# Merged cache runs, stacked new values and a finer last output in a hybrid attention decoder step

## The chip, the cores and the metric

The kernel runs on one core of a Trainium2 chip. The metric is the device time of one execution in microseconds, the median of several runs. TensorE (PE in the rows) multiplies matrices, ScalarE (ACT), VectorE (DVE) and GpSimd (POOL) work element by element, and SyncE (SP) issues nearly all transfers. The engines run side by side and wait for one another through semaphores.

## The reference

Two layers are applied to 320 tokens of width 1024: one prompt of 256, and eight samples of 8 tokens, each with a cache of 2048 earlier positions. Each layer does

```python
x = x + 0.5 * swiglu_1(rms(x))
z = rms(x) @ w_in                 # q, k, v of 3 dilated groups, of the sink attention, and 2 gates
A = dilated window attention      # (window, dilation) = (128,1), (512,4), (2048,16); 4 heads each,
                                  # the groups' heads weighted by their softmax denominators
B = window attention of 128       # 8 query heads on 2 key heads, with a learned sink per head
x = x + (sigmoid(gA) * (A @ w_branch_a) + sigmoid(gB) * (B @ w_branch_b)) @ w_out
x = x + 0.5 * swiglu_2(rms(x))
```

and after both a final norm follows. The attention of a sample goes over rows of its caches and over its 8 new keys and values. The outputs are y and all window caches, shifted by the new rows. All is in fp32.

## The kernel before, in words

Activations lie transposed, features on the partitions and 320 tokens along the free axis. A weight matrix is split into a rounded part and a rest (whi, wlo), as is the activation, and three matmuls of 320 columns make one product (L632 to L635). Weights come in units of eight 128x128 tiles: SP loads `raw` (L490), ACT rounds it (L1022), DVE takes the rest (L1244), and PE uses the unit. DVE's rest of unit n + 4 is made in step n, and SP loads the raw tile of unit v when the rest of unit v - 4 is done.

The mixer of a layer is written out by hand. `mixer_steps` (L118) makes one list of steps, and every engine walks it in order and does its share of each step. Step ("U", u) is unit u of w_in, 24 products on PE. `BEATS` (L111) says which pieces of attention follow unit u: S scores, T transposed probabilities, O values; the number is the item (0 to 3 prompt items of the dilated groups, 4 and 5 the sample items SA of these groups by half of the samples, 6 to 9 prompt items of the sink attention, 10 its sample item). S1a and S1b are two parts of a score. `TILES` (L114) says how many cache tiles follow unit u. There are 52 in a layer: 26 of keys (step K, `cached_keys`, 8 matmuls each) and 26 of values (step V, `cached_values`, 4 matmuls each), 13 for each half of the samples. They are small matmuls whose results have 32 rows, four of which lie side by side on the array.

The order in a step matters below. PE does unit u, then the beats, then the tiles. ACT empties the unit (`zs`, L1110), rounds a weight unit, copies transposed probabilities (L1179), and does the exponentials of a score (L1144) when DVE has found the maxima. POOL scales `zs` into `t1` (L1577). For a query or key unit DVE shuffles, multiplies and adds (L1334, L1338, L1341; the last signals `rope_done`). DVE also makes the maxima (L1410), the rest of a weight unit (step w) and the scaling of the exponentials (step N, L1442). Token rows of unit u - 3 (step R) are transposed in the middle of unit u, and ACT copies them out (L1122 to L1129).

Four waits of PE are named below. In the last key tile of the first half (tile 12, counted from 0) PE also multiplies the queries with the new keys, and for that it waits for the rotated keys of unit 14:

```python
if i == CT - 1 and half == 0:
    pe.wait_ge(rope_done, L * 17 + 12)       # L865
```

The first value tile of the second half (tile 39) waits until ACT has copied the sums of the first half out of PSUM, which is step Y, placed in the list behind tile 38:

```python
if half == 1 and i == 0:
    pe.wait_ge(osb_done, L * 2 + 1)          # L893
```

The values of an item of the dilated groups wait for the token rows of its value units (L811). And each tile waits for its load (`kvc_wait`). Loads go to a ring of `KV_RING` places; `cache_load_places` (L172) puts the load of tile n in SP's order seven units behind the step that uses tile n - KV_RING, and there SP waits until that tile is used.

The new values of the samples are summed in `values`: for an SA item 3 groups by 4 samples, 12 matmuls with 32 rows of `vnew` (L845). At the end DVE makes y in four parts of two of the eight feature chunks (L1513), and SP stores each (L620).

Of the kernel before, what the change touches and what calls it, by code (L numbers as in the profile page):

```python
# [7 lines left out]
F32 = mybir.dt.float32  # L8
# [5 lines left out]
P = 128  # L14
# [31 lines left out]

LOADS = (("x", 0), ("a", 0), ("x", 1), ("a", 1), ("x", 2), ("b", 0), ("x", 3), ("b", 1), ("w", 2), ("w", 3))
XPARTS = 4
HALF_UNIT = UT // 2 * P

START_RUNS = ((0, (0, 1)), (0, (2, 3)), (1, (0, 1, 2, 3)), (0, (4, 5)), (1, (4, 5)), (0, (6, 7)), (1, (6, 7)))
# [39 lines left out]
SA0 = ITEMS.index(("SA", 0, 0))  # L91
TWO_PARTS = [i for i, _i in enumerate(ITEMS) if _i[0] == "A" and _i[2] == 1]
SINKED = [i for i, _i in enumerate(ITEMS) if _i[0] in ("B", "SB")]
KV_RING = 5
KST = 3
T1 = 3
QK_GATES, QK_GATE0 = 12, 5
# [8 lines left out]
def parts(i):  # L106
# [1 line left out]

BEATS = {10: "S0", 12: "T0 S1a", 13: "S1b", 14: "O0", 15: "T1a", 16: "T1b S2", 18: "T2 O1 S3a", 19: "S3b", 20: "O2",  # L111
         21: "T3a", 22: "T3b S4", 23: "O3", 24: "T4 S5", 26: "T5 O4 S6", 27: "O5", 28: "T6 S7", 30: "T7 O6 S8",
         32: "T8 O7 S9", 34: "T9 O8 S10", 36: "T10 O9", 38: "O10"}
TILES = {10: 4, 12: 4, 14: 3, 16: 2, 18: 4, 20: 4, 22: 3, 23: 2, 26: 4, 28: 4, 30: 5, 32: 4, 34: 4, 36: 5}  # L114
FILL_Q = 6


# [122 lines left out]
def build(nc, a):  # L240
    ctx = ExitStack()
    with ctx:
# [37 lines left out]
        with ExitStack() as att:  # L280
            kvc = sb("kvc", [P, KV_RING, NB * P], F32, att)
            vb = sb("vb", [P, NB, P], F32, att)
            kb = sb("kb", [P, NB * P], F32, att)
            qm_mem = sb("qm_mem", [P, 2 * 4 * CT * HALF], F32, att)
            qk = sb("qk", [P, 17, TOK], F32, att)
            vtok = sb("vtok", [P, 2, 7 * P], F32, att)
            vnew = sb("vnew", [HALF, 2, 7 * P], F32, att)
            kst = sb("kst", [P, KST, 3 * P], F32, att)

            e = sb("e", [P, 2 * NG * SEQ], F32, att)
            pts = sb("pts", [P, 2 * NG * SEQ], F32, att)
            ptn = sb("ptn", [HALF, 4 * P], F32, att)

            sts = sb("sts", [P, N_SA], F32, att)
            osb = sb("osb", [P, 2 * P], F32, att)
            t1 = sb("t1", [P, T1, TOK], F32, att)
            cosr = sb("cosr", [P, TOK], F32, att)  # L300
            sinr = sb("sinr", [P, TOK], F32, att)
            mx = sb("mx", [P, 4], F32, att)
            nmx = sb("nmx", [P, 4], F32, att)
            den = sb("den", [P, 4], F32, att)
            esk = sb("esk", [P, 4], F32, att)
            nsk = sb("nsk", [P, 4], F32, att)
            rden = sb("rden", [P, 4], F32, att)
# [131 lines left out]
        def skips_first_rows(u):  # L439

            kind, g, _ = COLS[u]
            return kind == "k" and g in (0, 3)

        def new_place(first, count):

            return BK_T + 1, slice(first * P, (first + count) * P)
# [29 lines left out]
        def _(sp):  # L476
# [53 lines left out]
            def store_kv(L, n):  # L530

                kind, g, c = COLS[KV_UNITS[n]]
                name = ("a1", "a2", "a3", "b")[g]
                kv = 0 if kind == "k" else 1
                heads = P * c
                sp.wait_ge(kvtok_done, L * 14 + n + 1)
                if kind == "k":
                    nk = K_UNITS.index(KV_UNITS[n])
                    src, done = kst[:, nk % KST, 0:2 * P].rearrange("p (t f) -> p t f", t=2), kst_out[nk % KST]
                    parts = [(slice(0, NB), kst[0:NB * NT, nk % KST, 2 * P:3 * P])]  # L540
                else:
                    cols = slice(v_slot(g, c) * P, (v_slot(g, c) + 1) * P)
                    src, done = vtok[:, :, cols], v_out
                    parts = [(slice(4 * half, 4 * half + 4), vnew[:, half, cols]) for half in range(2)]
                t0 = 0 if g in (1, 2) else 1
                dst = a[f"new_{name}_prompt"].rearrange("l n (t p) v h d -> l p (n t) v (h d)", p=P)
                dst = dst[at(L), :, :, kv, heads:heads + P].rearrange("l p t f -> (l p) t f")
                sp.dma_start(dst, src[:, t0:2, :]).then_inc(done, 16)
                dst = a[f"new_{name}_sample"]
                w = dst.shape[2]  # L550
                dst = dst[:, :, w - NT:w, :, :, :].rearrange("l b t v h d -> l b t v (h d)")
                for batches, new in parts:
                    to = dst[at(L), batches, :, kv, heads:heads + P].rearrange("l b t f -> (l b) t f")
                    sp.dma_start(to, new).then_inc(done, 16)
# [55 lines left out]
            for L in range(DEPTH):  # L610
# [3 lines left out]
                    sp.dma_start(sinks[:, :, :], a["sinks"]).then_inc(const_in, 16)  # L614
                mixer_loads(L)
                ffn_loads(L, 1)
            for n in range(XPARTS):
                m = slice(n * KD // XPARTS, (n + 1) * KD // XPARTS)
                sp.wait_ge(y_done, m.stop)
                sp.dma_start(a["y"][:, m, :], x[:, m, :]).then_inc(y_out, 16)  # L620
            sp.wait_ge(y_out, 16 * XPARTS)
            sp.wait_ge(copy_out, 16 * DEPTH * (4 * 2 * NB + 2 * KD + 4 * 2))
            sp.wait_ge(v_out, DEPTH * 7 * 48)
            for n in range(KST):
# [4 lines left out]
        def _(pe):  # L629
# [89 lines left out]
            def mixer_products(L):  # L719
# [48 lines left out]
                def transposes(i, part):  # L768
# [13 lines left out]
                    elif kind == "B":  # L782
                        for n in range(4 * (t + 1)):
                            j, kt, cc = n // (2 * (t + 1)), n // 2 % (t + 1), n % 2
                            o = (2 * j + cc) * (t + 1) * P + kt * P
                            mm = pe.transpose(ps[:, BK_T + n // 4, n % 4 * P:(n % 4 + 1) * P], e[:, o:o + P], ident)
                    else:
                        for n in range(4 if kind == "SB" else NG):
                            o = n * N_SB if kind == "SB" else n * P
                            on = n * N_SB + P if kind == "SB" else NG * P + n * HALF  # L790
                            pe.transpose(ps[:, BK_T, n * P:(n + 1) * P], e[:, o:o + P], ident)
                            mm = pe.transpose(ps[0:HALF, *new_place(n, 1)], e[:, on:on + HALF], ident)
                    mm.then_inc(s_pt, 1)

                def values(i):
# [25 lines left out]
                    elif kind == "SB":  # L821
                        pe.wait_ge(vb_in, L * 16 + 16)
                        pe.wait_ge(kvtok_done, L * 14 + 14)
                        for h in range(2):
                            for j in range(2):
                                r, n = slice(HD * j, HD * (j + 1)), 2 * j + h
                                pe.matmul(ps[r, BK_O, h * P:(h + 1) * P],
                                          vnew[:, h, 6 * P + HD * j:6 * P + HD * (j + 1)],
                                          ptn[:, n * P:(n + 1) * P], start=True, stop=False)
                            for b in range(4):  # L830
                                for j in range(2):
                                    r, n = slice(HD * j, HD * (j + 1)), 2 * j + h
# [5 lines left out]
                    else:  # L838
# [1 line left out]
                        pe.wait_ge(s_masked, L * NI + SA0 + 2)  # L840
                        pe.wait_ge(kvtok_done, L * 14 + 12)
                        plain(pe)
                        for g in range(NG):
                            for b in range(4):
                                mm = pe.matmul(ps[HALF * b:HALF * (b + 1), BK_KV, 2 * P * c:2 * P * (c + 1)],  # L845
                                               ptn[:, g * P + HALF * b:g * P + HALF * (b + 1)],
                                               vnew[:, c, v_slot(g, 0) * P:(v_slot(g, 0) + 2) * P],
                                               start=g == 0 and c == 0, stop=False, skip_group_check=True)
                        mm.then_inc(s_new, 1)

                def cached_keys(n):
# [165 lines left out]
        def _(act):  # L1017
# [80 lines left out]
            def mixer_act(L):  # L1098
                act.wait_ge(const_in, 32)
                for kind, n in STEPS:  # L1100
# [11 lines left out]
                    elif kind == "R":  # L1112
# [12 lines left out]
                        else:  # L1125
                            v0 = v_slot(g, c) * P
                            nc.scalar.activation(vtok[:, :, v0:v0 + P],
                                                 ps[:, BK_ROWS, 0:2 * P].rearrange("p (t f) -> p t f", t=2), ACT.Copy)
                            nc.scalar.activation(vnew[:, :, v0:v0 + P],  # L1129
                                                 ps[0:HALF, BK_ROWS, 2 * P:4 * P].rearrange("p (t f) -> p t f", t=2),  # L1130
                                                 ACT.Copy).then_inc(kvtok_done, 1)
                    elif kind == "G":
                        k = G_UNITS.index(n)
                        act.wait_ge(t1_done, L * N_IN + n + 1)
# [14 lines left out]
                    elif kind == "T":  # L1149
# [5 lines left out]
                        if what == "SA":  # L1155
                            if h == 0:
                                act.wait_ge(pm_zero, L + 1)
                            else:
                                act.wait_ge(s_new, L * 2 + 1)
                            nc.scalar.activation(ptn[:, 0:NG * P], ps[0:HALF, *new_place(0, NG)], ACT.Copy)  # L1160
                            src = ps[:, BK_T, :]
                            by_tile = ((0, ((CT * HALF, 4), (1, HALF))),
                                       (HALF, ((CT * HALF, 4), (4, 2 * 4), (HALF + 1, 4))),
# [8 lines left out]
                        else:  # L1172
                            if part == 0 and users:
                                wait_item_out(act, L, users[-1])
                            if what == "SB":
                                act.wait_ge(s_new, L * 2 + 2)
                                nc.scalar.activation(ptn[:, :], ps[0:HALF, *new_place(0, 4)], ACT.Copy)
                            w = {"A": 2 * NG * P, "B": 4 * (t + 1) * P, "SB": 4 * P}[what]
                            nc.scalar.activation(pts[:, part * w:(part + 1) * w], flat[:, 0:w], ACT.Copy)\  # L1179
                                .then_inc(s_pts, 1)  # L1180
# [59 lines left out]
        def _(dve):  # L1240
# [267 lines left out]
                .then_inc(diag_done, 1)  # L1508
            dve.wait_ge(spread, 1)
            dve.wait_ge(xhi_done, (3 * DEPTH + 1) * KD)  # L1510
            for n in range(XPARTS):
                m = slice(n * KD // XPARTS, (n + 1) * KD // XPARTS)
                nc.vector.tensor_tensor(x[:, m, :], xg[:, m, :], strided(ps[:, BK_S, 0:TOK], 0, ((0, KD // XPARTS), (1, TOK))),  # L1513
                                        ALU.mult).then_inc(y_done, KD // XPARTS)


        @block.gpsimd
# [156 lines left out]
```

## Time and profile before

| | us |
|---|---|
| three runs | 1472.41, 1472.85, 1473.51 |
| median | 1472.85 |
| the profiled execution | 1472.82 |
| its span in the trace | 1471.0 |
| PE busy in the span | 1456.0 |
| DVE, ACT, POOL busy | 794.2, 668.7, 350.0 |

The profile page gives busy times, the span in forty slices, the chain of work that ended last, and the costliest groups. A row of a timeline gives the start, the duration, the engine, the line, the operation and how many instructions were merged (on PE, weight loads are counted in a merged row, so x64 is 32 matmuls), and in brackets how long the engine had stood idle and what released it. Matmuls overlap, so the distance of two starts says more than a duration.

### The profile page before, as it was taken

Reading aid. Unit: us, or ns where it says so; the run is one execution under the profiler, and the core shown is the slowest. Engines: PE = TensorE matmul, PEld = TensorE weight load, DVE = VectorE, ACT = ScalarE, POOL = GpSimd, SP = SyncE. Lnnn points to the kernel's source line nnn. Section 1 sums busy time; section 2 is a strip of 40 time slices with the busy share of each in tenths; the row PEclk is TensorE's granted clock in tenths of the full one; section 3 lists DMA queues with packets and bytes.
Section 4 is the critical chain, followed back from the end, with each engine's and each line's share of the span. In section 5 each row is a group of like instructions: output and inputs, shape, how many; then the busy total and the mean of one; then the engine's idle time right before and its main releaser. Section 6 shows DMA issues by size and latency. Waiting matters only on the chain.

```text
span 1471.0 us, 31019 instructions
## 1 busy us (share of the span) xinstructions
PE 1456.0 (99%) x11408; PEld 1415.5 (96%) x11408; DVE 794.2 (54%) x1281; ACT 668.7 (45%) x1109; POOL 350.0 (24%) x349
## 2 busy tenths in 40 slices
PE   9999999999999999999999999999999999999997
PEld 9999999999889999999999999999898899999997
DVE  5555445855445755544455554477554466555443
ACT  6444344444554544434454443444445445444342
POOL 1322212212115232220122221132121163222200
PEclk9999999999999999999999999999999999999999
DMA  8985566898674798547788846669877558885563
GB/s 311 349 287 177 168 202 201 320 325 283 226 257 135 249 330 295 178 137 206 221 314 293 293 147 183 202 203 334 287 262 273 183 169 293 310 290 156 156 195 112
DMA packets 94979, 349.80 MB, mean 238 GB/s; under 512 B 12336, under 2 KB 23856, under 8 KB 92208
## 3 DMA queue, kind: packets, MB, share of 16 engines
q1 hardware_dynamic: 94752, 348.64, 70.8%
q8 instruction: 55, 0.90, 0.3%
q14 instruction: 28, 0.23, 0.0%
q10 hardware_dynamic: 144, 0.03, 0.0%
HBM read 343.51 MB, written 94.37 MB: 298 GB/s over the span
## 4 chain that ended last, share of the span: by engine, by line
PE 93%; POOL 2%; DVE 2%; ACT 1%; issue 1%; DMA 0%; SPq 0%; DVEq 0%; ACTq 0%; POOLq 0%
PE ps L633 29%; PE ps L634 28%; PE ps L635 28%; PE ps L881 2%; PE ps L895 2%; POOL ma L1582 1%; PE ps L817 1%; PE ps L732 1%; PE ps L781 1%; POOL mlo L1585 0%; PE ps L742 0%; DMA x<-in_x 0%; PE ps L806 0%; ACT whi L1022 0%; PE ps L845 0%
## 5 line engine op out<-in xcount | busy, mean ns | idle before, releaser
L1244 DVE TENSOR_TENSOR wlo<-raw,whi 128x1024 fp32r<-128x1024 f32 (+2 forms) x414 | 485.4, 1173 | 381.7 <-ACT whi L1022 381.3
L633 PE MATMUL ps<-xhi,whi 128*128 128x320 f32 x2048 | 641.7, 313 | 1.0 <-DVE wlo L1482 0.6
L635 PE MATMUL ps<-xhi,wlo 128*128 128x320 f32 x2048 | 632.7, 309 | 0.0
L634 PE MATMUL ps<-xlo,whi 128*128 128x320 f32 x2048 | 632.6, 309 | 0.0
L1022 ACT ACTIVATE whi<-raw 128x1024 fp32r<-128x1024 f32 (+2 forms) x414 | 397.7, 963 | 304.7 <-PE ps L635 300.6
L633 PEld LDWEIGHTS ps<-xhi,whi 128*128 128x128 f32 x2048 | 384.4, 188 | 12.6 <-issue 9.8
L634 PEld LDWEIGHTS ps<-xlo,whi 128*128 128x128 f32 x2048 | 384.6, 188 | 0.5
L635 PEld LDWEIGHTS ps<-xhi,wlo 128*128 128x128 f32 x2048 | 384.4, 188 | 0.0
L633 PE MATMUL ps<-act_hi,whi 128*128 128x320 f32 x704 | 217.5, 309 | 0.0
L634 PE MATMUL ps<-act_lo,whi 128*128 128x320 f32 x704 | 217.5, 309 | 0.0
L635 PE MATMUL ps<-act_hi,wlo 128*128 128x320 f32 x704 | 217.5, 309 | 0.0
L1538 POOL TENSOR_TENSOR up_s<-gate_s,up_s 128x320 f32<-128x320 f32 x88 | 86.1, 979 | 392.3 <-DVE up_s L1284 366.8
L633 PEld LDWEIGHTS ps<-act_hi,whi 128*128 128x128 f32 x704 | 132.1, 188 | 0.0
L634 PEld LDWEIGHTS ps<-act_lo,whi 128*128 128x128 f32 x704 | 132.1, 188 | 0.0
L635 PEld LDWEIGHTS ps<-act_hi,wlo 128*128 128x128 f32 x704 | 132.1, 188 | 0.0
L1531 POOL TENSOR_TENSOR ssq<-ssq,sq 128x320 f32<-128x320 f32 x47 | 47.5, 1012 | 302.2 <-ACT sq L1044 242.0
L1064 ACT ACTIVATE gate_s<-gate_s 128x320 f32<-128x320 f32 x88 | 41.4, 471 | 159.3 <-DVE gate_s L1284 159.3
L1542 POOL TENSOR_TENSOR act_lo<-up_s,act_hi 128x320 f32 x88 | 87.5, 994 | 69.1 <-ACT act_hi L1073 69.1
L1577 POOL TENSOR_TENSOR t<-zs,rinv 128x320 f32<-128x320 f32 x46 | 43.2, 940 | 211.3 <-ACT zs L1110 211.3
L1110 ACT ACTIVATE zs<-ps 128x320 f32<-128x320 f32 x80 | 35.0, 437 | 127.6 <-PE ps L635 127.5
L1284 DVE TENSOR_TENSOR gate_s<-ps,rinv 128x320 f32<-128x320 f32 x88 | 43.2, 491 | 81.5 <-PE ps L635 81.4
L1073 ACT ACTIVATE act_hi<-up_s 128x320 f32 (+1 forms) x88 | 41.6, 473 | 67.7 <-POOL up_s L1538 67.7
(154 smaller groups left out, 1194.9 us busy)
## 6 DMA issues: line engine op xcount, KB each, us to landing
out_new_a_sample<-in_cache_a SPq DMA_DIRECT2D x128, 510.0 KB, 5.3
raw<-in_ffn_gate SPq DMA_DIRECT2D x87, 512.0 KB, 3.7
raw<-in_ffn_up SPq DMA_DIRECT2D x87, 512.0 KB, 4.5
raw<-in_w_in SPq DMA_DIRECT2D x80, 512.0 KB, 5.3
kvc<-in_kcache SPq DMA_DIRECT2D x52, 512.0 KB, 6.5
kvc<-in_vcache SPq DMA_DIRECT2D x52, 512.0 KB, 5.5
raw<-in_ffn_down SPq DMA_DIRECT2D x64, 384.0 KB, 3.2
raw<-in_ffn_down SPq DMA_DIRECT2D x64, 320.0 KB, 3.0
```

The lines of the kernel that those rows point to most:

```text
L633: pe.matmul(out, w0, hi, start=first, stop=False)
L634: pe.matmul(out, w0, lo, start=False, stop=False)
L635: return pe.matmul(out, w1, hi, start=False, stop=last)
L1022: nc.scalar.activation(whi[:, (base + s) % RING, 0:tiles * P], raw[:, (base + s) % RAW, 0:tiles * P], ACT.Copy).then_inc(whi_done, 1)
L1064: nc.scalar.activation(gate_s[:, s // 2, :], gate_s[:, s // 2, :], ACT.Silu)\
L1073: nc.scalar.activation(dst, up_s[:, s // 2, :], ACT.Copy).then_inc(acthi_done, 1)
L1244: nc.vector.tensor_tensor(wlo[:, (base + s) % RING, 0:tiles * P], raw[:, (base + s) % RAW, 0:tiles * P], whi[:, (base + s) % RING, 0:tiles ...
L1284: nc.vector.tensor_tensor((gate_s, up_s)[s % 2][:, s // 2, :], ps[:, s, 0:TOK], rinv[:, :], ALU.mult).then_inc(taken, 1)
L1531: nc.gpsimd.tensor_tensor(ssq[:, :], ssq[:, :], sq[:, slot, :], ALU.add).then_inc(ssq_done, 1)
L1538: nc.gpsimd.tensor_tensor(up_s[:, q, :], gate_s[:, q, :], up_s[:, q, :], ALU.mult)\
L1542: nc.gpsimd.tensor_tensor(chunk(act_lo, j), up_s[:, q, :], chunk(act_hi, j).bitcast(F32), ALU.subtract).then_inc(actlo_done, 1)
L1577: nc.gpsimd.tensor_tensor(t1[:, n % T1, :], zs[:, n % 2, :], by[:, :], ALU.mult).then_inc(t1_done, 1)
```

## The change

Five edits are made together.

1. The new values of the three groups lie under one another on partitions 0 to 95 (`vnew` [96, 2, 256], with `vnb` for the sink attention), and so do the transposed probabilities (`ptn` [96, 512]). The SA items then use 4 matmuls with 96 rows in place of 12 with 32 rows.
2. The probabilities of the new keys are transposed for the three groups at once, in one transpose of 96 columns in place of three of 32.
3. The values of items 0, 2 and 5 follow units 15, 21 and 28, behind the transposes there, in place of units 14, 20 and 27.
4. The 52 cache tiles follow 11 units in place of 14, and the ring has 6 places in place of 5.
5. y is made and stored in parts of 3, 2, 2 and 1 chunks.

```diff
+YPARTS = ((0, 3), (3, 5), (5, 7), (7, 8))
-KV_RING = 5
+KV_RING = 6
-BEATS = {10: "S0", 12: "T0 S1a", 13: "S1b", 14: "O0", 15: "T1a", 16: "T1b S2", 18: "T2 O1 S3a", 19: "S3b", 20: "O2",
-         21: "T3a", 22: "T3b S4", 23: "O3", 24: "T4 S5", 26: "T5 O4 S6", 27: "O5", 28: "T6 S7", 30: "T7 O6 S8",
+BEATS = {10: "S0", 12: "T0 S1a", 13: "S1b", 15: "T1a O0", 16: "T1b S2", 18: "T2 O1 S3a", 19: "S3b",
+         21: "T3a O2", 22: "T3b S4", 23: "O3", 24: "T4 S5", 26: "T5 O4 S6", 28: "T6 O5 S7", 30: "T7 O6 S8",
          32: "T8 O7 S9", 34: "T9 O8 S10", 36: "T10 O9", 38: "O10"}
-TILES = {10: 4, 12: 4, 14: 3, 16: 2, 18: 4, 20: 4, 22: 3, 23: 2, 26: 4, 28: 4, 30: 5, 32: 4, 34: 4, 36: 5}
+TILES = {10: 5, 12: 4, 14: 4, 18: 5, 20: 4, 22: 4, 26: 5, 28: 5, 30: 6, 32: 5, 34: 5}
...
-            vnew = sb("vnew", [HALF, 2, 7 * P], F32, att)
+            vnew = sb("vnew", [NG * HALF, 2, 2 * P], F32, att)
+            vnb = sb("vnb", [HALF, 2, P], F32, att)
...
-            ptn = sb("ptn", [HALF, 4 * P], F32, att)
+            ptn = sb("ptn", [NG * HALF, 4 * P], F32, att)
...
+        def new_rows(g, c):
+            return vnew[HALF * g:HALF * (g + 1), :, c * P:(c + 1) * P] if g < NG else vnb[:, :, :]
...
-            for n in range(XPARTS):
-                m = slice(n * KD // XPARTS, (n + 1) * KD // XPARTS)
+            for part in YPARTS:
+                m = slice(*part)
                 sp.wait_ge(y_done, m.stop)
                 sp.dma_start(a["y"][:, m, :], x[:, m, :]).then_inc(y_out, 16)
...
-                            on = n * N_SB + P if kind == "SB" else NG * P + n * HALF
                             pe.transpose(ps[:, BK_T, n * P:(n + 1) * P], e[:, o:o + P], ident)
-                            mm = pe.transpose(ps[0:HALF, *new_place(n, 1)], e[:, on:on + HALF], ident)
+                            if kind == "SB":
+                                mm = pe.transpose(ps[0:HALF, *new_place(n, 1)], e[:, o + P:o + N_SB], ident)
+                        if kind == "SA":
+                            mm = pe.transpose(ps[0:NG * HALF, *new_place(0, 1)], e[:, NG * P:N_SA], ident)
...
-                        for g in range(NG):
-                            for b in range(4):
-                                mm = pe.matmul(ps[HALF * b:HALF * (b + 1), BK_KV, 2 * P * c:2 * P * (c + 1)],
-                                               ptn[:, g * P + HALF * b:g * P + HALF * (b + 1)],
-                                               vnew[:, c, v_slot(g, 0) * P:(v_slot(g, 0) + 2) * P],
-                                               start=g == 0 and c == 0, stop=False, skip_group_check=True)
+                        for b in range(4):
+                            mm = pe.matmul(ps[HALF * b:HALF * (b + 1), BK_KV, 2 * P * c:2 * P * (c + 1)],
+                                           ptn[:, HALF * b:HALF * (b + 1)], vnew[:, c, :],
+                                           start=c == 0, stop=False, skip_group_check=True)
...
-                            nc.scalar.activation(vnew[:, :, v0:v0 + P],
+                            nc.scalar.activation(new_rows(g, c),
...
-                            nc.scalar.activation(ptn[:, 0:NG * P], ps[0:HALF, *new_place(0, NG)], ACT.Copy)
+                            nc.scalar.activation(ptn[:, 0:P], ps[0:NG * HALF, *new_place(0, 1)], ACT.Copy)
...
-            for n in range(XPARTS):
-                m = slice(n * KD // XPARTS, (n + 1) * KD // XPARTS)
-                nc.vector.tensor_tensor(x[:, m, :], xg[:, m, :], strided(ps[:, BK_S, 0:TOK], 0, ((0, KD // XPARTS), (1, TOK))),
-                                        ALU.mult).then_inc(y_done, KD // XPARTS)
+            for m0, m1 in YPARTS:
+                m = slice(m0, m1)
+                nc.vector.tensor_tensor(x[:, m, :], xg[:, m, :], strided(ps[:, BK_S, 0:TOK], 0, ((0, m1 - m0), (1, TOK))),
+                                        ALU.mult).then_inc(y_done, m1 - m0)
```

In the new list tile 12 follows unit 14 (before: unit 16), the new keys of the second half follow unit 22 (before: unit 23), and tile 39 lies inside the run behind unit 30 (before: first in the run behind unit 32).

## Rows read from the trace of the kernel before

**Rows 1.** The page, busy time, share of the span and instructions by engine.

```profile
PE 1456.0 (99%) x11408; PEld 1415.5 (96%) x11408; DVE 794.2 (54%) x1281; ACT 668.7 (45%) x1109; POOL 350.0 (24%) x349
```

**Rows 2.** Who waited for whom, PE: total, times, longest.

```profile
PE ps L817 <- ACT vnew L1129: 3.0, 4, 1.4
```

**Rows 3.** Timeline of PE, layer 0, behind unit 14: values of item 0, tiles.

```profile
306.97 0.31 PE L635 MATMUL ps<-xhi,wlo 128*128 128x320 f32 x1
308.59 0.88 PE L817 MATMUL ps<-pts,vtok 128*64 128x128 f32 x12 [1.30 <-ACT vnew L1129]
309.39 1.52 PE L881 MATMUL ps<-kvc,qm_mem 128*32 128x128 f32 x48
310.84 0.41 PE L633 MATMUL ps<-xhi,whi 128*128 128x320 f32 x1
```

**Rows 4.** Timeline of PE, layer 0, behind unit 26.

```profile
376.62 1.50 PE L845 MATMUL ps<-vnew,ptn 32*32 32x256 f32 x24
378.05 0.71 PE L742 MATMUL ps<-qk 64*128 64x128 f32 x8
378.69 1.93 PE L895 MATMUL ps<-kvc,qm_mem 128*32 128x256 f32 x32
380.55 0.42 PE L633 MATMUL ps<-xhi,whi 128*128 128x320 f32 x1
```

**Rows 5.** Timeline of PE and ACT, both layers, behind unit 30.

```profile
402.10 2.37 PE L895 MATMUL ps<-kvc,qm_mem 128*32 128x256 f32 x40
404.40 0.41 PE L633 MATMUL ps<-xhi,whi 128*128 128x320 f32 x1
...
405.30 0.36 ACT L1191 ACTIVATE osb<-ps 128x256 f32<-128x256 f32 x1
...
1127.10 2.37 PE L895 MATMUL ps<-kvc,qm_mem 128*32 128x256 f32 x40
...
1130.29 0.36 ACT L1191 ACTIVATE osb<-ps 128x256 f32<-128x256 f32 x1
```

**Rows 6.** Timeline of PE, layer 0, transposes of item 4.

```profile
368.61 0.27 PE L791 MATMUL ps<-const,e 128*128 128x128 f32 x1
368.72 0.27 PE L792 MATMUL ps<-const,e 128*32 128x128 f32 x1
```

**Rows 7.** Timeline of PE, layer 0: last products of unit 13, scores behind it.

```profile
301.82 0.31 PE L634 MATMUL ps<-xlo,whi 128*128 128x320 f32 x1
301.96 0.31 PE L635 MATMUL ps<-xhi,wlo 128*128 128x320 f32 x1
302.20 0.94 PE L732 MATMUL ps<-qk 64*128 64x128 f32 x12
```

**Rows 8.** Timeline of ACT and DVE, layer 0, behind unit 14.

```profile
308.08 0.36 ACT L1129 ACTIVATE vnew<-ps 32x256 f32<-32x256 f32 x1
...
310.41 0.49 DVE L1341 TENSOR_TENSOR qk<-t,sq 128x320 f32<-128x320 f32 x1
```

**Rows 9.** Timeline of PE and DVE, layer 1, behind unit 14.

```profile
1033.57 0.88 PE L817 MATMUL ps<-pts,vtok 128*64 128x128 f32 x12 [1.42 <-ACT vnew L1129]
...
1035.40 0.49 DVE L1341 TENSOR_TENSOR qk<-t,sq 128x320 f32<-128x320 f32 x1
```

**Rows 10.** Cache loads behind units 10 (four) and 30 (five), from line L579.

```profile
DMA to landing us min/median/max: 8.1/9.3/10.4
...
DMA to landing us min/median/max: 3.6/5.3/8.2
```

**Rows 11.** The last parts of y: timeline of DVE, landing from line L620.

```profile
1465.10 3.01 DVE L1513 TENSOR_TENSOR x<-wide,ps 128x640 f32<-128x640 f32 x4 [1.32 <-PE ps L1013]
...
DMA to landing us min/median/max: 2.2/2.4/2.5
```

**Rows 12.** Busy time by stretch: length, engines, TensorE's granted clock, DMA.

```profile
1032.00:1036.00 4.00, 2.58 (x63) 2.09 (x62) 3.01 (x9) 2.85 (x7) 1.19 (x1) 1.00 1.04 384
...
1465.50:1467.00 1.50, 0.00 (x0) 0.00 (x0) 1.50 (x3) 0.00 (x0) 0.00 (x0) 0.53 0.14 55
```

More of the change, by code:

```diff
@@ L543, in store_kv @@
                     src, done = vtok[:, :, cols], v_out
-                    parts = [(slice(4 * half, 4 * half + 4), vnew[:, half, cols]) for half in range(2)]
+                    parts = [(slice(4 * half, 4 * half + 4), new_rows(g, c)[:, half, :]) for half in range(2)]
                 t0 = 0 if g in (1, 2) else 1
@@ L616, in _ @@
                 ffn_loads(L, 1)
-            for n in range(XPARTS):
-                m = slice(n * KD // XPARTS, (n + 1) * KD // XPARTS)
+            for part in YPARTS:
+                m = slice(*part)
                 sp.wait_ge(y_done, m.stop)
                 sp.dma_start(a["y"][:, m, :], x[:, m, :]).then_inc(y_out, 16)
-            sp.wait_ge(y_out, 16 * XPARTS)
+            sp.wait_ge(y_out, 16 * len(YPARTS))
             sp.wait_ge(copy_out, 16 * DEPTH * (4 * 2 * NB + 2 * KD + 4 * 2))
@@ L827, in values @@
                                 pe.matmul(ps[r, BK_O, h * P:(h + 1) * P],
-                                          vnew[:, h, 6 * P + HD * j:6 * P + HD * (j + 1)],
-                                          ptn[:, n * P:(n + 1) * P], start=True, stop=False)
+                                          vnb[:, h, HD * j:HD * (j + 1)],
+                                          ptn[0:HALF, n * P:(n + 1) * P], start=True, stop=False)
                             for b in range(4):
@@ L1128, in mixer_act @@
                                                  ps[:, BK_ROWS, 0:2 * P].rearrange("p (t f) -> p t f", t=2), ACT.Copy)
-                            nc.scalar.activation(vnew[:, :, v0:v0 + P],
-                                                 ps[0:HALF, BK_ROWS, 2 * P:4 * P].rearrange("p (t f) -> p t f", t=2),
-                                                 ACT.Copy).then_inc(kvtok_done, 1)
+                            nc.scalar.activation(new_rows(g, c),
+                                                 ps[0:HALF, BK_ROWS, 2 * P:4 * P].rearrange(
+                                                     "p (t f) -> p t f", t=2), ACT.Copy).then_inc(kvtok_done, 1)
                     elif kind == "G":
@@ L1176, in mixer_act @@
                                 act.wait_ge(s_new, L * 2 + 2)
-                                nc.scalar.activation(ptn[:, :], ps[0:HALF, *new_place(0, 4)], ACT.Copy)
+                                nc.scalar.activation(ptn[0:HALF, :], ps[0:HALF, *new_place(0, 4)], ACT.Copy)
                             w = {"A": 2 * NG * P, "B": 4 * (t + 1) * P, "SB": 4 * P}[what]
```

## The prediction

> **What bounds the kernel now.** Look first at the busy times: PE is busy for 1456.0 of 1471.0 us, the next engine for 794.2 [rows 1]. So time goes only by what PE must do, and by the moments in which PE stands still. Next comes the table of waits, for PE alone. It is short, and its largest entry is 3.0 us in four waits, the longest 1.4: the values of items 0 and 2 (in two layers each) wait for token rows that ACT copies late [rows 2]. Third, the timeline of PE at such a place, read by the distance of starts. Behind unit 14 the last product starts at 306.97, the values of item 0 at 308.59, after 1.30 us of idle time [rows 3]. What edits 1 to 4 change is PE's work between units; the question is what each removes from PE's list, and whether a wait that was hidden comes to light when pieces of that list move.
>
> **New values (edit 1).** Twelve matmuls take 378.05 - 376.62 = 1.43 us [rows 4]. Four are left, with more rows and the same 256 columns. A value tile is four matmuls of that shape, and it costs the difference between a run of five and one of four: (404.40 - 402.10) - (380.55 - 378.69) = 2.30 - 1.86 = 0.44 us [rows 4, 5]. A third of 1.43 is 0.48. I take 0.48, so 0.95 saved; two items in two layers give 3.8 us. Bounds: 3.4 (if a group of four pays some 0.1 us more to get in and out) to 4.0. Nothing on PE hides this work, so the whole of it counts. ACT's copy of the probabilities gets shorter too, but PE does not wait for it.
>
> **Transposes (edit 2).** They follow one another every 0.11 us [rows 6]. Two fewer in each of four items: 0.9 us, all on the path.
>
> **Moved values (edit 3).** The copy that items 0 and 2 wait for is made about one unit before they now run, so the four waits go. Two products follow each other by 0.14, and a group of small matmuls starts 0.24 behind the last product [rows 7], so without its wait item 0 would have started at 306.97 + 0.24 = 307.21, not 308.59: 1.38 us [rows 3]. In layer 1 the idle time is 0.12 longer: 1.50 [rows 9]. The two others have 3.0 - 1.30 - 1.42 = 0.28 together. Sum: 3.2 us. What is late next is ACT's copy of the following transposes, which now waits for these values. It starts some 1.9 us behind the unit and takes 0.8, and the token rows that need the bank come half a unit after the next one has begun, later than that by about 0.8 us: no wait.
>
> **Eleven runs (edit 4), the boundaries.** Three tiles take 310.84 - 309.39 = 1.45 = 3 x 0.44 + 0.13 [rows 3]; five value tiles 5 x 0.44 + 0.10 [rows 5]. So a run costs some 0.1 us beside its tiles, and up to 0.10 more (0.24 against 0.14) where it stands alone behind a unit. Three runs fewer and item 5 no longer alone save 0.3 to 0.7 us in a layer. Items 0 and 2, which led into a run of tiles, now come behind full transposes and pay their own way in and out, as do the runs that they left: 0.2 to 0.6 back. I take nothing, with 0.5 us in a layer to either side. The tiles themselves, 52, and the products with new keys are the same in number.
>
> **What the moves expose: tile 12.** It is the last key tile of the first half, and PE first waits there for the rotated keys of unit 14 (L865). Before, it stood behind unit 16. Now it is the fourth tile behind unit 14 itself. The keys cannot be had sooner: ACT is held by the exponentials of item 1, then copies token rows (until 308.08 + 0.36 = 308.44) and only then empties unit 14; POOL and DVE follow, and DVE's last addition ends at 310.41 + 0.49 = 310.90 [rows 8]. None of this depends on what was moved. A signal needs 308.59 - 308.44 = 0.15 us from ACT to PE [rows 3, 8]; I take the same from DVE. PE begins the run at 307.21, reaches tile 12 at 307.21 + 3 x 0.44 = 308.53, and goes on at 311.05: 2.5 us of new idle time. In layer 1 the run would begin at 1033.57 - 1.50 = 1032.07, reach tile 12 at 1033.39, and the keys are there at 1035.89 + 0.15 = 1036.04: 2.65 [rows 9]. Sum 5.2. The new wait is longer than the one that edit 3 takes away at the same place. Behind it in PE's queue is unit 15, and everything. ACT's copy of the scores and DVE's second set of queries are held as well, but they are used behind unit 18. DVE's rest of unit 18, moved behind these copies, has more than two units to spare.
>
> **Tile 39.** The first value tile of the second half waits until ACT has copied the first half's sums (L893). In the old list tile 39 opens the run behind unit 32, long after that copy. In the new list unit 30 has six tiles, 36 to 41, so it is the fourth of a run, and the copy can be asked for only when tile 38 has ended. ACT's list has the exponentials of item 8 before the copy; it runs at 405.30 and ends at 405.66 [rows 5]. That is set by the scores of item 8, which stay where they are. Tile 39 would start at 402.10 + 3 x 0.44 = 403.42 and can go at 405.66 + 0.15 = 405.81: 2.4 us. Layer 1: 1127.10 + 1.32 = 1128.42 against 1130.29 + 0.36 + 0.15 = 1130.80, again 2.4. Sum 4.8. For both new waits the bounds are 1.2 us each (were the work ahead of them half as long) and 3 us (ACT or DVE a little more loaded).
>
> **Loads.** A ring of six lets each run find its first tiles loaded earlier, but more loads now follow one run: five behind units 10 and 28, six behind unit 30. Old rows show up to 10.4 us from issue to landing behind unit 10, up to 8.2 for five loads behind unit 30 [rows 10]. The tightest new case is tile 41: issued 0.2 us behind the run of unit 28, wanted two units (2 x 24 x 0.14 = 6.7), some 2 us of beats, five tiles (2.2) and the wait at tile 39 (2.4) later, some 13 us. It is in time by 3 us even at 10.4. Cost nothing; if it failed, its wait would be one of 1 to 3 us.
>
> **The end (edit 5).** DVE's four multiplications move the same 2560 columns in about the same 3.0 us; the last transfer is half as large, and landed 2.2 to 2.5 us after issue at full size [rows 11]. I take 0.2 us saved, between 0 and 0.5.
>
> **Sum.** -3.8 - 0.9 - 3.2 + 0 + 5.2 + 4.8 - 0.2 = +1.9 us. The profiled execution took 1472.82 us, 1.8 more than its span and within 0.03 of the median 1472.85, so the forecast is 1474.7 by either.
>
> **The rivals.**
> *One wait is hidden.* If the keys of unit 14 or the copy for tile 39 came in time, 5.2 or 4.8 us would drop out: 1469.5 to 1469.9. For it speaks that both estimates rest on work of other engines in the old order; against it, that nothing ahead of that work is removed. *Neither wait is paid:* 1464.7, with both judgements wrong.
> *Slower, by late loads.* The larger groups of loads share the queue with weights and copies. This decides once a tile behind units 10, 28 or 30 lands more than 13 us after its issue; the old worst is 10.4 [rows 10]. A wait of 1.5 us at one such run in each layer gives 1474.7 + 3.0 = 1477.7.
> *Slower, by the clock.* While PE had 1.42 us of idle time within a stretch the granted clock stayed at 1.00 (2.4 GHz); at the very end, after PE had done only a few small matmuls with gaps, it went to half (0.53 over a stretch in which it fell) [rows 12]. The new idle times of 2.4 to 2.65 us lie between. If it fell at one, up to one unit of 24 x 0.14 = 3.4 us would run at half speed, 3.4 us more (an estimate, no product stands in the trace at the lower level); for four, 1474.7 + 13.6 = 1488.3. The Trainium skill, "TensorE: Matmul & The Clock Gate", Part 1, says that the throttled clock is the default and that idleness brings it back, which speaks against every new idle time; the trace agrees at its end and not at 1.42 us.
>
> **Chances.** Both waits paid, nothing else: 0.63, range 1473 to 1476.5. One hidden: 0.13. Neither: 0.05. Late loads: 0.15. Clock: 0.04. A measurement of this kernel can tell about 0.2%, 2.9 us, from no change, so "same" is 1469.9 to 1475.8. The main case lies within it but for some 0.06 above. Slower is 0.15 + 0.04 + 0.06 = 0.25; faster is 0.13 + 0.05 less the part of the first that ends above 1469.9: 0.15; same 0.60. The range from 1469.5 to 1477.0 holds the main case, one hidden wait and half of the late loads.
>
> **What would show it.** Right: PE has no wait for token rows at L817; L845 takes about 0.5 us for four matmuls; at L875 PE waits 2.5 us for DVE L1341 in each layer, and in the middle of the run behind unit 30 2.4 us for ACT L1191. Wrong: PE goes through either place without idle time, waits for a cache load at L881 or L895, or the granted clock falls inside a layer.

## The result, and the profile after

The changed kernel takes 1477.79 us (median of 7, 1477.11 to 1479.61) against 1472.85 (1472.41 to 1473.51): 0.35% slower, ratio 1.0035 with a 95% interval of 1.0024 to 1.0046. Forecast were 1474.7 and a range to 1477.0. The profiled execution took 1478.36 us, its span is 1476.6.

Line numbers after the change are some six higher (L881 is now the products with new keys, L887 and L901 the key and value tiles). The first two views are the page's busy times, which stand beside [rows 1], and the table of waits of PE, beside [rows 2].

```profile
PE 1455.7 (99%) x11336; PEld 1416.7 (96%) x11336; DVE 797.2 (54%) x1281; ACT 668.8 (45%) x1109; POOL 348.3 (24%) x349
```

```profile
PE ps L881 <- DVE qk L1347: 4.7, 2, 2.4
PE ps L901 <- ACT osb L1197: 4.4, 2, 2.2
```

The wait for token rows is gone, and two new ones are there, of the forecast sizes. Both can be seen in the timelines. First PE (layer 0, then layer 1) and DVE (layer 0) behind unit 14, beside [rows 3, 8, 9]:

```profile
307.17 0.31 PE L641 MATMUL ps<-xhi,wlo 128*128 128x320 f32 x1
307.40 1.52 PE L887 MATMUL ps<-kvc,qm_mem 128*32 128x128 f32 x48
311.23 0.59 PE L881 MATMUL ps<-qk,qm_mem 128*32 128x32 f32 x46 [2.30 <-DVE qk L1347]
...
312.22 0.42 PE L639 MATMUL ps<-xhi,whi 128*128 128x320 f32 x1
...
1034.66 1.52 PE L887 MATMUL ps<-kvc,qm_mem 128*32 128x128 f32 x48
1038.61 0.59 PE L881 MATMUL ps<-qk,qm_mem 128*32 128x32 f32 x46 [2.43 <-DVE qk L1347]
```

```profile
309.97 0.58 DVE L1344 TENSOR_TENSOR sq<-sq,sinr 128x320 f32<-128x320 f32 x1
310.59 0.49 DVE L1347 TENSOR_TENSOR qk<-t,sq 128x320 f32<-128x320 f32 x1
```

Three tiles, then 2.30 us of idle time (2.43 in layer 1); DVE has written the rotated keys at 311.08, and PE goes on at 311.23. Next PE (both layers) and ACT (layer 0) behind unit 30, beside [rows 5]:

```profile
401.29 1.50 PE L901 MATMUL ps<-kvc,qm_mem 128*32 128x256 f32 x24
404.98 1.94 PE L901 MATMUL ps<-kvc,qm_mem 128*32 128x256 f32 x24 [2.19 <-ACT osb L1197]
406.85 0.64 PE L639 MATMUL ps<-xhi,whi 128*128 128x320 f32 x1
...
1128.66 1.50 PE L901 MATMUL ps<-kvc,qm_mem 128*32 128x256 f32 x24
1132.36 2.27 PE L901 MATMUL ps<-kvc,qm_mem 128*32 128x256 f32 x24 [2.19 <-ACT osb L1197]
1134.56 0.64 PE L639 MATMUL ps<-xhi,whi 128*128 128x320 f32 x1
```

```profile
404.00 0.38 ACT L1150 ACTIVATE e<-e,nmx 128x128 f32<-128x128 f32 x1
...
404.38 0.19 ACT L1153 ACTIVATE esk<-nsk 128x4 f32<-128x4 f32 x1
404.48 0.36 ACT L1197 ACTIVATE osb<-ps 128x256 f32<-128x256 f32 x1
```

Three tiles, 2.19 us of idle time until ACT has done the exponentials (the last at L1150, then a small one at L1153) and then the copy, three tiles. The next product has a duration of 0.64 us where the same row of before had 0.41 [rows 5]. That is the sign of what the forecast missed, and the busy times by stretch show it (PEclk, the granted clock, is the third number from the end; three stretches around and behind the wait at tile 39 in layer 0, the one behind it in layer 1, then the wait at tile 12 of layer 0 and what follows it):

```profile
402.70:405.90 3.20, 1.01 (x24) 0.71 (x24) 2.78 (x11) 2.37 (x11) 0.00 (x0) 1.00 0.94 291
405.90:409.30 3.40, 3.40 (x21) 2.59 (x14) 0.22 (x1) 0.00 (x0) 0.00 (x0) 0.50 1.06 377
409.30:412.00 2.70, 2.70 (x21) 2.70 (x20) 0.00 (x0) 0.23 (x1) 0.00 (x0) 1.00 0.91 329
1132.95:1136.35 3.40, 3.40 (x27) 2.33 (x16) 0.55 (x3) 0.00 (x0) 0.00 (x0) 0.50 1.05 388
308.90:311.20 2.30, 0.02 (x4) 0.00 (x1) 2.11 (x6) 1.26 (x2) 0.92 (x1) 1.00 1.05 398
311.30:314.70 3.40, 3.40 (x81) 3.20 (x82) 2.23 (x21) 0.77 (x3) 0.00 (x0) 1.00 1.02 413
```

Behind the wait at tile 39 the clock is at half (1.2 GHz) for 3.4 us in both layers, although PE is busy throughout; behind the wait at tile 12 it stayed at 1.00 in this execution. At the lower level products follow one another by 0.27 us, at the upper by 0.15, in the timeline of unit 31 (layer 0; the last row is the first transpose behind the unit):

```profile
407.81 0.47 PE L639 MATMUL ps<-xhi,whi 128*128 128x320 f32 x1
408.08 0.47 PE L640 MATMUL ps<-xlo,whi 128*128 128x320 f32 x1
...
410.26 0.31 PE L639 MATMUL ps<-xhi,whi 128*128 128x320 f32 x1
410.40 0.31 PE L640 MATMUL ps<-xlo,whi 128*128 128x320 f32 x1
...
411.58 0.38 PE L912 MATMUL ps<-const,osb 128*128 128x128 f32 x2
```

The three tiles behind the wait took 1.87 us (404.98 to 406.85), where the same three behind the same wait take 1.43 at full clock (layer 1 of e1, below). Unit 31 took 4.73 (406.85 to 411.58) against 3.62 before: 404.40 [rows 5] to

```profile
408.02 0.38 PE L906 MATMUL ps<-const,osb 128*128 128x128 f32 x2
```

So this fall of the clock cost 1.5 us, and that of layer 1, reckoned in the same way, 1.6.

The pieces that got cheaper, behind unit 26, beside [rows 4, 6] (PE's timeline):

```profile
376.31 0.49 PE L796 MATMUL ps<-const,e 128*128 128x128 f32 x3
376.63 0.27 PE L800 MATMUL ps<-const,e 128*96 128x128 f32 x1
376.84 0.64 PE L852 MATMUL ps<-vnew,ptn 96*32 96x256 f32 x8
377.40 0.71 PE L748 MATMUL ps<-qk 64*128 64x128 f32 x8
```

Four transposes for six, and four matmuls in 0.56 us for twelve in 1.43. Last the loads behind unit 28 and the stores of y, beside [rows 10, 11]:

```profile
DMA to landing us min/median/max: 3.6/6.3/8.3
...
DMA to landing us min/median/max: 2.6/2.8/2.8
```

The loads are in time: no row of the waits names one. The stores of y land later, not sooner, than before (2.2 to 2.5). The last matmul and DVE's multiplications stand in the timeline of the end as

```profile
1468.40 1.44 PE L1019 MATMUL ps<-diag,ones 80*128 80x320 f32 x2 [1.15 <-DVE diag L1511]
1470.30 3.01 DVE L1519 TENSOR_TENSOR x<-wide,ps 128x960 f32<-128x960 f32 x4 [1.95 <-PE ps L1019]
```

From DVE's start to the end of the span are 1476.6 - 1470.30 = 6.3 us, before 1471.0 - 1465.10 = 5.9 [rows 11]. The last matmul has 1.44 us here; in the trace of before it had 0.81:

```profile
1463.83 0.81 PE L1013 MATMUL ps<-diag,ones 80*128 80x320 f32 x2 [1.15 <-DVE diag L1505]
```

### The profile page after: what moved, and what is told of

Its sections match the earlier page's. It is cut to its first block, busy times and chain, and to the rows that moved or that the text cites. A ratio compares the mean times of both kernels' runs of the same rounds, so it can differ in the third digit from the quotient of the medians.

```text
span 1476.6 us, 30875 instructions
## 1 busy us (share of the span) xinstructions
PE 1455.7 (99%) x11336; PEld 1416.7 (96%) x11336; DVE 797.2 (54%) x1281; ACT 668.8 (45%) x1109; POOL 348.3 (24%) x349
## 4 chain that ended last, share of the span: by engine, by line
PE 93%; DVE 2%; POOL 2%; issue 1%; ACT 1%; DMA 0%; SPq 0%; DVEq 0%; ACTq 0%; POOLq 0%
PE ps L639 29%; PE ps L640 28%; PE ps L641 28%; PE ps L901 2%; PE ps L887 1%; POOL ma L1588 1%; PE ps L825 1%; PE ps L738 1%; PE ps L787 1%; POOL mlo L1591 0%; PE ps L748 0%; DMA x<-in_x 0%; PE ps L814 0%; ACT whi L1028 0%; PE ps L792 0%
```

## The experiments

Every time is a median, with the lowest and highest of its executions in brackets; "before" was run beside each.

**Tiles 9 to 12 behind unit 15 (e1).**

```diff
-TILES = {10: 5, 12: 4, 14: 4, 18: 5, ...
+TILES = {10: 5, 12: 4, 15: 4, 18: 5, ...
```

> The changed kernel with one edit: the four tiles 9 to 12 follow unit 15 in place of unit 14, so that the rotated keys of unit 14 are ready when tile 12 needs them. Theory (two waits, and a fall of the clock behind the second): the idle time before L881, 4.7 us in two layers, goes, the wait at L901 and the half clock behind it stay; 1477.8 - 4.7 = 1473.1. Rival (the wait only moves): DVE's second set of queries comes as much later as the tiles, and tile 13 behind unit 18 waits instead; 1477 to 1478.

Measured: 1470.51 (1469.03 to 1473.22, 11 executions), ratio to before 0.9988 (0.9979 to 0.9997). The wait at L881 is gone and none took its place; that at L901 is still 4.4 us. The gain is larger than the 4.7 us of the wait. Busy times by stretch behind the wait at tile 39, layer 0 and layer 1, and PE's timeline there in layer 1:

```profile
402.50:405.80 3.30, 3.30 (x28) 2.05 (x18) 0.78 (x4) 0.00 (x0) 0.00 (x0) 0.50 0.97 343
...
1126.00:1129.00 3.00, 2.23 (x29) 1.61 (x30) 1.49 (x8) 0.98 (x5) 0.00 (x0) 1.00 1.02 419
```

```profile
1126.77 1.50 PE L901 MATMUL ps<-kvc,qm_mem 128*32 128x256 f32 x24 [2.19 <-ACT osb L1197]
1128.20 0.42 PE L639 MATMUL ps<-xhi,whi 128*128 128x320 f32 x1
```

Here the clock fell once, in layer 0, and not in layer 1 behind the same wait. So the fall is not certain, and the theory that it comes at every wait was too simple; the spread of 4 us over equal executions says the same.

**Scores of item 8 behind tile 38 (e2).** PE does them while ACT, no longer held by their exponentials, copies the sums. A word of BEATS that ends with "!" is kept back until step Y.

```diff
-... 30: "T7 O6 S8",
+... 30: "T7 O6 S8!",
...
+                (late if word.endswith("!") else steps).append((word[0], (i, part)))
...
                 steps.append(("Y", SA0 + tile // CT - 3))
+                steps += late
+                late = []
```

> The changed kernel with one edit: the scores of item 8 stand behind tile 38 in place of ahead of tile 36, so that ACT copies the first half's sums before the exponentials of item 8 and PE has the scores to do meanwhile. Theory (the idle time before tile 39 brings the clock down): 4.4 us of idle time and 2 x 1.7 us of half clock go, 0.2 us are paid for one more way into a run; 1470.2, granted clock 1.00 through both layers. Rival (the long run of small matmuls brings the clock down, not the idle time): only the 4.4 us go, the clock still falls behind unit 30; 1473.6.

Measured: 1470.34 (1470.08 to 1473.17, 11 executions), 0.9989 (0.9980 to 0.9998). The waits of PE, first row:

```profile
PE ps L883 <- DVE qk L1349: 4.7, 2, 2.4
```

The wait at tile 39 is gone, the clock is 1.00 through both layers of the profiled execution, and all six tiles still follow unit 30, with the scores in their middle. But four of the eleven executions took 1471.8 to 1473.2, and their mean granted clock was 0.995 or 0.996, that of the seven others 0.997. The wait at tile 12 is the only one of this length left, so behind it the clock can fall as well.

**Both (e3).**

> The changed kernel with both edits, tiles 9 to 12 behind unit 15 and the scores of item 8 behind tile 38. Theory: both waits and the half clock go; 1477.8 - 4.7 - 4.4 - 3.4 + 0.2 = 1465.5, which is faster than before by 7.3. Rival (waits move to the loads or to DVE once these are gone): PE waits at L887 or L901 for a load, 1468 to 1471.

Measured: 1464.81 (1464.39 to 1465.07, 5 executions), 0.9945 (0.9931 to 0.9958). No wait of PE within the layers is longer than 0.3 us, the spread is 0.7 us, and the mean granted clock is 0.998 in all five executions, although the six tiles still follow unit 30: these small matmuls do not bring the clock down by themselves. The difference to e2, 5.5 us, is what the wait at tile 12 costs in the median, and that to e1, 5.7, what the wait at tile 39 costs, falls of the clock included. The two do not add up to the 13.0 us between e3 and the changed kernel; the clock falls in some executions and not in others, and medians of such spreads do not add.

**The second wait filled (e4), both filled (e5).** The waits stay, PE multiplies meanwhile (e4 has the first piece of the diff, e5 both); nothing of the result comes from these products, and their bank and weights are waited for ahead of them.

```diff
                     if half == 1 and i == 0:
...
+                        for _ in range(14):
+                            pe.matmul(ps[:, 1, 0:TOK], whi[:, 31 % RING, 0:P], xhi[:, 0, :], start=True, stop=True)
                         pe.wait_ge(osb_done, L * 2 + 1)
...
                     if i == CT - 1 and half == 0:
...
+                        for _ in range(15):
+                            pe.matmul(ps[:, 1, 0:TOK], whi[:, 15 % RING, 0:P], xhi[:, 0, :], start=True, stop=True)
                         pe.wait_ge(rope_done, L * 17 + 12)
```

> The changed kernel with 14 products (320 columns, results thrown away) put before the wait at tile 39, into the bank that unit 31 overwrites; the wait itself stays. 14 x 0.147 = 2.06 us, against 2.2 us of idle time. Theory (the idle time brings the clock down): PE is as late as before, but the clock stays at 1.00; 1477.8 - 3.4 = 1474.4. Rival (the clock falls for another reason, such as the long runs of small matmuls or the load of the other engines): no change, 1477.8.

Measured: 1475.86 (1475.06 to 1477.95, 8 executions), 1.0023 (1.0013 to 1.0034). The profiled execution, the fastest, has the clock at 1.00 as long as PE works (0.998 in the mean). In five of the seven others the mean was 0.995 or 0.996: the clock fell at the wait that was left.

> The changed kernel with both waits kept and filled: 14 thrown-away products before the wait at tile 39, and 15 before the wait at tile 12. Theory (idle time of PE is what lets the clock fall, at either wait, in some executions and not in others): PE is as late as with the waits, but the clock stays at 1.00 in all executions; 1475 to 1476 in each, spread under 1 us. Rival (the long runs of small matmuls, or the transfers beside them, let it fall): the times spread over 1475 to 1479, as with the second wait alone filled.

Measured: 1474.95 (1474.25 to 1475.59, 11 executions), 1.0015 (1.0006 to 1.0024). All executions lie within 1.4 us, and around both places the clock is at 1.00 in both layers (busy times by stretch, layer 0):

```profile
306.00:312.00 6.00, 6.00 (x136) 5.41 (x136) 4.08 (x9) 3.98 (x8) 0.93 (x1) 1.00 1.06 394
...
406.00:412.00 6.00, 6.00 (x51) 5.61 (x40) 0.17 (x2) 1.75 (x5) 0.89 (x1) 1.00 0.97 364
```

PE goes on as late as in the changed kernel (the products with new keys start at 311.21, there at 311.23), yet the kernel is 2.8 us faster, by work that nobody needs. So with the idle time the falls are gone, while loads, long runs and the small matmuls are all still there.

The mean granted clock of every execution says the same (3.4 us at half take 1.7 of 1473 us, some 0.001, off it). It was 0.997 or 0.998 wherever no new wait stood idle (every execution of the kernel before that was run beside an experiment, and every one of e3 and of e5 to e10). It was 0.994 to 0.996 in all seven executions of the changed kernel, and 0.995 or 0.996 in four of eleven of e1, four of eleven of e2 and five of eight of e4.

**Edits 1 and 2 alone (e6), edit 3 alone (e7), edit 5 alone (e8)**, each on the kernel before, with the lines of the change as they stand in its diff.

> The kernel before with edits 1 and 2 alone (stacked new values, one transpose). A group of four matmuls took 0.57 us in the changed kernel, twelve 1.43: 4 x 0.86 = 3.4, and the transposes 0.9; 1472.7 - 4.3 = 1468.4. Rival (part of it comes back as idle time, since the values of items 0 and 2 still wait): 1470 to 1472.

Measured: 1468.87 (1468.26 to 1469.37, 8 executions), 0.9974 (0.9963 to 0.9984): 3.9 us less. The waits of PE, first row:

```profile
PE ps L825 <- ACT vnew L1135: 3.5, 4, 1.5
```

4.3 us of work are gone, 0.5 came back as a longer wait for token rows.

> The kernel before with edit 3 alone (values of items 0, 2, 5 moved; 14 runs, ring of five). Theory: the four waits of 3.2 us go, and some 0.2 us in a layer come back at boundaries; 1472.7 - 2.8 = 1469.9. Rival (the idle time goes elsewhere, to the copy that now waits for the values): 1472 to 1473.

Measured: 1469.61 (1469.12 to 1470.42, 11 executions), 0.9980 (0.9971 to 0.9989): 3.1 us less, and no wait of PE in a layer above 0.3 us.

> The kernel before with edit 5 alone (y in parts of 3, 2, 2, 1). As predicted: 0.2 us less, 1472.5. Rival, from the changed kernel's last 6.3 us against 5.9 before: the smaller transfer lands no sooner (2.6 to 2.8 against 2.2 to 2.5 us), and 0.3 to 0.4 us are lost, 1473.0.

Measured: 1473.11 (1472.56 to 1473.78, 11 executions), 1.0003 (0.9994 to 1.0012). The interval holds 1, so the times show neither sign. The stores landed 2.6 to 2.9 us after issue, as in the changed kernel. The end in this trace, with the layers as before:

```profile
1462.84 1.43 PE L1014 MATMUL ps<-diag,ones 80*128 80x320 f32 x2 [1.15 <-DVE diag L1506]
1464.73 3.01 DVE L1514 TENSOR_TENSOR x<-wide,ps 128x960 f32<-128x960 f32 x4 [1.95 <-PE ps L1014]
```

From DVE's start to the end of the span are 1471.0 - 1464.73 = 6.3 us. It is 6.2 to 6.3 in all eight traces with uneven parts and 5.9 to 6.0 in the four with equal ones: uneven parts lose some 0.3 us there, which the times are too coarse to show. The slow last matmul (1.43 us) stands here too, without any new wait, and in e7 (1.34): it differs between executions and does not come from the change.

**The changed kernel without edit 4 (e9, first diff), and e3 with equal parts of y (e10, second diff).**

```diff
-KV_RING = 6
+KV_RING = 5
-TILES = {10: 5, 12: 4, 14: 4, 18: 5, 20: 4, 22: 4, 26: 5, 28: 5, 30: 6, 32: 5, 34: 5}
+TILES = {10: 4, 12: 4, 14: 3, 16: 2, 18: 4, 20: 4, 22: 3, 23: 2, 26: 4, 28: 4, 30: 5, 32: 4, 34: 4, 36: 5}
```

```diff
-YPARTS = ((0, 3), (3, 5), (5, 7), (7, 8))
+YPARTS = ((0, 2), (2, 4), (4, 6), (6, 8))
```

> The changed kernel without edit 4: 14 runs of tiles and a ring of five, all other edits. Tile 12 then follows unit 16 and tile 39 opens the run behind unit 32, so neither new wait is there. Theory (merging the runs is worth nothing by itself, edit 4 brings the waits): no idle time, clock at 1.00, 1472.7 - 3.4 - 0.9 - 2.8 = 1465.6. Rival (eleven runs save what they were counted to, 0.5 us in a layer): 1 us slower than the kernel with both waits taken away, 1465.9 against 1464.9.

Measured: 1465.55 (1464.88 to 1465.80, 5 executions), 0.9951 (0.9937 to 0.9965). Without edit 4 the change would have been 7 us faster than before; edit 4 as it was made turns that into 4.9 slower, some 12 us in all. Eleven runs without the waits (e3, 1464.81) are 0.7 us faster than fourteen; the two intervals overlap.

> The changed kernel with tiles 9 to 12 behind unit 15 and the scores of item 8 behind tile 38, and y in four equal parts as before. If the uneven parts cost 0.4 us: 1464.4. If they save 0.2: 1465.0. It is also the candidate for the best of these kernels.

Measured: 1464.89 (1464.57 to 1465.31, 5 executions), 0.9948 (0.9935 to 0.9962): the same as e3. The parts of y make no difference that these times show.

## Why the prediction was wrong

The sum held, the assumption under it did not. With its idle times filled so that the clock stays up (e5), the changed kernel takes 1474.95 us; the forecast was 1474.7. That the two are so close is in part luck: the errors of the terms below nearly cancel. The steps, one by one:

- *New values*, 0.95 each: 0.86 to 0.87 measured. A group of four took 0.56 to 0.57, not 0.48; the way in and out of a small group was the bound that I named.
- *Transposes*, 0.9 in all, and *moved values*, 3.2: right. Edits 1 and 2 together gave 3.9 us (e6, with 0.5 given back to a wait), edit 3 by itself 3.1 (e7).
- *Boundaries*, nothing taken with 0.5 us a layer to either side: 0.7 us saved in both layers together by e9 against e3, within the bound.
- *Tile 12*, 2.5 and 2.65; *tile 39*, 2.4 each. The forecast counted from the moment at which the tile would have started, three tiles of 0.44 behind the start of its run. By that measure tile 12 was late by 311.23 - 307.40 - 1.32 = 2.51 us and in layer 1 by 2.63, tile 39 by 2.37 and 2.38: 9.9 in all, and 10.0 were forecast. (The idle times of the rows, 2.30, 2.43 and 2.19 twice, begin only when the matmuls ahead have ended.) Right in place, releaser and size; e5, which keeps the waits, is 10.1 us slower than e3, which has neither.
- *Loads*, nothing: right.
- *The end*, 0.2 saved: the wrong sign. The traces with uneven parts have some 0.3 us more from DVE's start to the end (6.2 to 6.3 against 5.9 to 6.0, e8); the times show neither sign.
- *The clock*: this is the step that failed. The text said that the new idle times "lie between" the 1.42 us that had not moved the clock and the end of the kernel where it fell, and gave a fall 0.04. In the profiled execution it fell behind both waits at tile 39, 3.1 us together. That is the sign of being wrong which the prediction had named. The price was off as well: 3.4 us a fall by my bound, 1.5 to 1.6 measured, since half of a 3.4 us stretch is lost, not a whole unit. In the medians the falls are the 2.8 us between the changed kernel and e5. At the end of the kernel the last matmul ran at 0.50 in this execution and at full clock in that of before, 0.6 more (1.44 us against 0.81); as e7 and e8 show, this is not of the change.

So the rival called "slower, by the clock" is what happened, on top of the main case. The profiled execution adds up: 9.9 us of new waits, 3.1 and 0.6 of clock and 0.4 in the last stores, less 7.5 of work and old waits and 0.7 of boundaries, give 5.8; measured 1478.36 - 1472.82 = 5.5. Under the forecast lay an argument from one row, 1.42 us without a fall [rows 12], to waits 1.7 to 1.9 times as long. It spoke for no fall at 1.42 us and said nothing about 2.4. The kernel before had no idle time of PE in a layer beyond 1.42 us in its trace, and its executions lie within 1.8 us (1472.23 to 1474.02, the widest set). The Trainium skill, "TensorE: Matmul & The Clock Gate", Part 1, had the rule that idleness brings the throttled clock back, and here the traces agree at 2.2 us behind tile 39, in both layers of the changed kernel and in one of the two of e1.

Open: what decides, in an execution, whether the clock falls. The same wait of 2.2 us did it in one layer of e1 and not in the other. The wait of 2.3 to 2.4 at tile 12 did not in the profiled executions of the changed kernel, e2 and e4; the granted clocks of e2 and e4 show that it does in others, but no profile here has such a fall in it. Whether idle time would do it without small matmuls on either side is not shown: ahead of the falls behind tile 39 in the changed kernel PE was busy for 1.0 of 3.2 us, and the products that filled the waits raised that share as they took the idle time away.

## What to carry to other kernels

When a list of work written by hand is regrouped, ask of every piece that moves ahead, or comes to stand inside a group, which wait it carries: two waits that cost nothing in their old places made 13 us of difference (e3 against the changed kernel), and both went by changing the order of two items. Idle times of TensorE of 2.2 to 2.4 us cost more than their length here, in some executions of e1, e2 and e4 and in all of the changed kernel. Where a forecast has idle time longer than any that the old trace shows to be harmless, take a fall of the clock as a likely case, not as a rare one, and look for work to do meanwhile. And where executions of one kernel spread over several microseconds while its neighbour's agree within one, look at the granted clock before anything else.

## What was not expected of the hardware

- The clock came back after 3.4 us at half in every fall seen inside a layer (two here, one in e1), with PE busy all the while.
- Adding 58 products that nobody uses made the kernel 2.8 us faster (1474.95 against 1477.79), with PE held as late at both places.
- The store of one eighth of y after one of a quarter landed no sooner: 2.6 to 2.9 us from issue, against 2.2 to 2.5 for four equal stores.
